# The first norm of a two-layer transformer kernel: row parts by TensorE and VectorE in turn, bias rows ahead of x, four units tile by tile

## What is computed

```python
cond = jax.nn.silu(c)                                     # (1, 1024)
mod = (cond @ ada_w[l] + ada_b[l]).reshape(B, 3, 3, 1, D) # shift, scale, gate of 3 sublayers
h = rms_norm(x, norm_g[l, 0]) * (1 + mod[:, 0, 1]) + mod[:, 0, 0]
a, b = jnp.split(h @ ffn1_w13[l], 2, axis=-1)
x = x + 0.5 * mod[:, 0, 2] * ((jax.nn.silu(a) * b) @ ffn1_w2[l])
wl = jnp.einsum("bqhd,bkd->bhqk", qb, kwb) + t5_table[t5_bucket(wd)].transpose(2, 0, 1)
```

## Time and profile before

| | |
|---|---|
| Median of three runs | 3389.39 us |
| Profiled execution | 3389.15 us, span 3387.4 us |
| TensorE | 98% of the span busy |
| VectorE, ScalarE, GpSimd | 67%, 39%, 13% |
| DMA | 380.90 MB, mean 112 GB/s |
| Granted TensorE clock | 0.997 of full |

### The profile page before, as it was taken

The page is one execution under the profiler, slowest core; times in us unless marked ns, Lnnn a source line. Parts: engine busy times, 40 slices in busy tenths (PEclk is TensorE's granted clock), DMA queues, the critical chain, the costliest instruction groups (busy, mean ns, idle before and its releaser), DMA issues. The chain is left out here.

```text
span 3387.4 us, 51035 instructions
## 1 busy us (share of the span) xinstructions
PE 3329.7 (98%) x19808; PEld 2811.7 (83%) x19808; DVE 2267.5 (67%) x3615; ACT 1317.6 (39%) x2095; POOL 438.0 (13%) x329
## 2 busy tenths in 40 slices
PE   8999999999999999999999999999999999999999
PEld 7989877788888898987778888886888888788887
DVE  6877757658775677785765877657666525766642
ACT  5424344535333433334453523243443324443321
POOL 2000200222000300020022200121200011120002
PEclk9999999999999999999999999999999999999999
DMA  6463523113542345442201353321233332223332
GB/s 252 148 229 129 166 86 94 32 39 127 176 145 96 112 154 211 144 150 88 87 26 54 128 192 124 101 77 52 81 99 99 105 102 63 68 82 94 96 104 85
DMA packets 88629, 380.90 MB, mean 112 GB/s; under 512 B 9774, under 2 KB 10926, under 8 KB 77192
## 3 DMA queue, kind: packets, MB, share of 16 engines
q1 hardware_dynamic: 88456, 378.52, 33.5%
HBM read 376.36 MB, written 2.12 MB: 112 GB/s over the span
## 5 line engine op out<-in xcount | busy, mean ns | idle before, releaser
L2001 DVE TENSOR_TENSOR wL<-wR,wH 128x1024 fp32r<-128x1024 f32 (+2 forms) x160 | 207.9, 1299 | 195.4 <-ACT wH L1289 195.2
L1289 ACT ACTIVATE wH<-wR 128x1024 fp32r<-128x1024 f32 (+2 forms) x158 | 175.0, 1107 | 381.3 <-PE bank L3452 305.6
L3697 PE MATMUL bank<-hH,wH 128*128 128x512 f32 x640 | 271.6, 424 | 0.0
L3566 PE MATMUL bank<-gHc,wH 128*128 128x512 f32 x660 | 256.8, 389 | 0.0
L3567 PE MATMUL bank<-gHc,wL 128*128 128x512 f32 x660 | 256.8, 389 | 0.0
L3568 PE MATMUL bank<-gLc,wH 128*128 128x512 f32 x660 | 256.7, 389 | 0.0
L3699 PE MATMUL bank<-hL,wH 128*128 128x512 f32 x640 | 251.6, 393 | 0.0
L3539 PE MATMUL bank<-hH,wH 128*128 128x512 f32 x640 | 249.7, 390 | 1.2 <-DVE wL L2057 1.2
L3698 PE MATMUL bank<-hH,wL 128*128 128x512 f32 x640 | 250.5, 391 | 0.0
L3540 PE MATMUL bank<-hH,wL 128*128 128x512 f32 x640 | 249.4, 390 | 0.0
L3541 PE MATMUL bank<-hL,wH 128*128 128x512 f32 x640 | 249.0, 389 | 0.0
(11 more groups left out here) (567 smaller groups left out, 8683.0 us busy)
## 6 DMA issues: line engine op xcount, KB each, us to landing
RW<-in_ffn_wq SPq DMA_DIRECT2D x80, 1024.0 KB, 5.6
adaw<-in_ada_w SPq DMA_DIRECT2D x144, 512.0 KB, 4.4
wR<-in_w_up SPq DMA_DIRECT2D x88, 512.0 KB, 3.6
wR<-in_ffn_w SPq DMA_DIRECT2D x56, 704.0 KB, 4.1
wR<-in_w_mix SPq DMA_DIRECT2D x72, 512.0 KB, 3.6
wR<-in_w_down SPq DMA_DIRECT2D x32, 704.0 KB, 4.1
wR<-in_w_in SPq DMA_DIRECT2D x40, 512.0 KB, 3.6
ada<-in_ada_first SPq DMA_DIRECT2D x8, 1024.0 KB, 12.1
```

Of the source, the lines that this page charges most:

```text
L3566: pe.matmul(o, wh[:, k, :], gHc[:, k, c], start=k == 0, stop=False)
L3697: pe.matmul(o, wH[n][:, k, :], hH[:, k, :], start=k == 0, stop=False)
```

## The change

The order of the queue: constants and `cond`, the small tensors, and only then x and the parameters; parts 0 and 1, units 0 and 1, part 2, the bias rows, parts 3 and 4, unit 2, part 5, unit 3, part 7, the first quarter, `SKEW`, part 6, the second quarter, `CSKEW`. The bias rows are made before x is transposed. Of the eight parts TensorE sums four (0, 2, 4, 6) and VectorE four (1, 3, 5, 7). TensorE's way is `part_sums` (eight matmuls of 32 rows out by 256 columns, four of them beside each other in PSUM), a copy by ScalarE, and `part_columns` (two matmuls of one column). VectorE adds squares in pairs, so that TensorE makes four row sums of 512 columns instead of sixteen of 256, and copies half of the transposed x. The norm goes tile by tile, over all 512 positions, each with its own bias and scale; the products of all four units follow tile by tile. The table matmuls stand between tiles 5 and 6. The fillers are gone. On ScalarE `sum_high(0)` moves behind the copies for the first quarter.

```diff
@@ SyncE
-            sp.dma_start(xin[:, :, :], a["x"].rearrange("(t p) d -> p t d", p=P)).then_inc(S.x_in, 16)
             sp.dma_start(cond[:, :], bc(a["c"], [P, D])).then_inc(S.const_in, 16)
...
             sp.dma_start(FLIP[:, :], a["c_flip"]).then_inc(S.tab_in, 16)
+            sp.dma_start(xin[:, :, :], a["x"].rearrange("(t p) d -> p t d", p=P)).then_inc(S.x_in, 16)
+            sp.dma_start(par[:, 0:C_END1], a["par1"][0]).then_inc(S.par_in, 16)
...
+                    ada_part(5)
+                    unit(ubase + 3, w13[l, 3], KT, 1)
+                    ada_part(7)
+                    sp.wait_ge(S.dc, 2)
+                    pair(f, 0, wq, l)
+                    sp.wait_ge(S.bias_out, 32)
+                    sp.wait_ge(S.ada0_done, 1)
+                    sp.dma_start(SKEW[:, :, :], bass.AP(bias_dram.tensor, 0, [[1, P], [640, H], [1, T]])).then_inc(S.skew_in, 16)
+                    ada_part(6)
+                    sp.wait_ge(S.ada0_done, 2)
+                    pair(f, 1, wq, l)
+                    sp.wait_ge(S.dc, 4)
                     sp.wait_ge(S.ada0_done, 4)
-                elif f:
...
+                    sp.wait_ge(S.skew_in, 16)
                     sp.dma_start(CSKEW[:, :, :], bass.AP(cbias_dram.tensor, 0, [[1, P], [1056, H], [1, 896]])).then_inc(S.skew_in, 16)
@@ ScalarE
+                first_high(0)
+                first_high(1)
+                first_sums(0)
+                act.wait_ge(S.ms, 1)
+                act.activation(rstd[:, :], bank[MS_BANK[0]][:, :], ACT.Ln, bias=eps, scale=1.0 / D).then_inc(S.ln, 2)
...
+                act.activation(rstd[:, :], rstd[:, :], ACT.Exp, scale=-0.5).then_inc(S.rstd, 2)
+                first_sums(1)
+                for k in range(KT):
+                    for e, c in enumerate(HALVES):
+                        act.wait_ge(S.hf, 2 * k + e + 1)
+                        act.activation(hH[:, k, c], HB[e][k // TT][:, k % TT, :], ACT.Identity,
+                                       bias=mod[:, k:k + 1]).then_inc(S.h_hi, 1)
+                    if k == 1:
+                        first_high(2)
+                    if k == 2:
+                        first_sums(2)
+                    if k == 4:
+                        first_high(3, fourth)
+                    if k == 5:
+                        first_sums(3)
+                        bias_tables()
@@ VectorE
+                for i in range(TT - 1):
+                    square_pair(i)
+                first(FIRST_DVE[0])
+                square_pair(TT - 1)
+                low(0)
+                low(1)
...
+                part(0)
+                part(1)
+                normed(0)
+                normed(1)
+                normed_low(0)
+                normed_low(1)
+                part(2)
+                normed(2)
+                normed_low(2)
+                first(3)
...
+                part(6)
+                normed(6)
+                first(7)
+                normed_low(6)
+                part(7)
+                normed(7)
+                normed_low(7)
@@ TensorE
+            pe.wait_ge(S.ct, 2)
+            pe.wait_ge(S.bias_sb, 1)
             pe.wait_ge(S.x_in, 16)
...
+            def part_sums(i):
...
+                for r in range(2):
+                    for g in range(4):
+                        mm = pe.matmul(bank[DS_BANK[i % 2]][32 * g:32 * (g + 1), 0:2 * P], CT[:, 4 * r + g, :], rows[:, 4 * r + g, :],
+                                       start=r == 0, stop=r == 1)
...
+            part_sums(0)
+            for i in range(TT):
+                pe.wait_ge(S.sq_sum, i + 1)
+                mm = pe.matmul(bank[MS_BANK[0]][:, :], ones, squares[2 * i], start=i == 0, stop=i == TT - 1)
+            mm.then_inc(S.ms, 2)
+            part_columns(0)
+            part_sums(1)
+            pe.wait_ge(S.rstd, 2)
+            part_columns(1)
...
+                both(0)
+                both(1)
+                part_sums(2)
+                both(2)
+                part_columns(2)
+                both(3)
+                pe.wait_ge(S.w_lo, 3)
+                tiles(2, 0, 4)
+                both(4)
+                tiles(2, 4, 5)
+                part_sums(3)
+                both(5)
+                part_columns(3)
+                pe.wait_ge(S.mod0, 2 * FIRST_PE[3] + 1)
+                bias_tables()
+                pe.wait_ge(S.w_lo, 4)
+                tiles(2, 5, 6)
+                tiles(3, 0, 6)
+                both(6)
+                both(7)
+                tiles(2, 6, 8)
+                tiles(3, 6, 8)
...
-                    warm(24)
-                    pe.wait_ge(S.mod_set, at(S.mod_set, 2))
-                    warm(3)
```

More of the change, by code:

```diff
@@ L333 @@
 SUMS = slice(3 * P, 3 * P + TT)
-ADA_PARTS = tuple((2 * c, 2 * c + 2) for c in range(KT))
+FIRST_TILES = (26, 30, 34, 38, 8, 12)
+FIRST_PE = (0, 2, 4, 6)
+FIRST_DVE = (1, 3, 5, 7)
 FIRST_COUNTS = {"w_in0": 688, "w_in1": 688, "w_hi": 86, "w_lo": 86, "w_used": 86, "sil": 4, "g_mul": 4, "g_hi": 44,
@@ L1162, in ffn @@
             def ffn(f, ubase, udn, l, w13, wq, w2, n, c, c_end):
[L1164 to L1170, removed]
+                if f == 0 and l == 0:
+                    for k in range(2):
+                        ada_part(k)
+                    for k in range(2):
+                        sp.dma_start(wR[k][:, 0:KT, :], w13[l, k]).then_inc(S.w_in[k], 16)
+                    ada_part(2)
                     sp.wait_ge(S.bias_sb, 1)
@@ L2166, in chunk, with ffn @@
                 g_low(f, q1)
-            def ffn(f, sub, n, ubase, udn, gates, ahead, part, rest=None):
+            def ffn(f, sub, n, ubase, udn, gates, ahead, part, rest=None, start=False):
                 def pair_out(i, b):
@@ new lines, in part_columns @@
+            def part_columns(i):
+                if i == 0:
+                    pe.wait_ge(S.picks, 2)
+                if i >= 2:
+                    pe.wait_ge(S.mod0, 2 * FIRST_PE[i - 2] + 1)
+                pe.wait_ge(S.ds, 2 * i + 2)
+                for j in range(2):
+                    mm = pe.matmul(bank[DC_BANK[i % 2]][:, j:j + 1], DS[i % 2][:, j * P:(j + 1) * P], picks[:, :], start=True, stop=True)
+                mm.then_inc(S.dc, 1)
+            pe.wait_ge(S.x_copied, TT)
+            pe.wait_ge(S.x_moved, TT)
@@ L3477, in open_three, with first_four, part, tiles @@
                         part(2, e, k)
+            def first_four():
+                def part(u, k):
+                    wh, wl = FIRST_W[u] if u < 3 else next(w for k0, k1, w in fourth if k0 <= k < k1)
+                    j = k if u < 3 else next(k - k0 for k0, k1, w in fourth if k0 <= k < k1)
+                    o = bank[u][:, :]
+                    pe.matmul(o, wh[:, j, :], hH[:, k, :], start=k == 0, stop=False)
+                    pe.matmul(o, wl[:, j, :], hH[:, k, :], start=False, stop=False)
+                    mm = pe.matmul(o, wh[:, j, :], hL[:, k, :], start=False, stop=k == KT - 1)
+                    if k == KT - 1:
+                        mm.then_inc(S.w_used, 1)
+                def tiles(u, k0, k1):
+                    for k in range(k0, k1):
+                        pe.wait_ge(S.h_lo, 2 * k + 2)
+                        part(u, k)
+                def both(k):
+                    tiles(0, k, k + 1)
+                    tiles(1, k, k + 1)
+                pe.wait_ge(S.w_lo, 2)
+                both(0)
[20 more added lines that the diff above has]
+                tiles(3, 6, 8)
             def products_third(o):
@@ L3569, in rows, with chunk @@
                 return mm
-            def chunk(f, u, half, xdone, xbase, ss=None):
+            def chunk(f, u, half, xdone, xbase, ss=None, between=None):
                 if half:
@@ L3578, in chunk @@
                 else:
+                    if between:
+                        pe.wait_ge(S.bm_set, H)
                     classical(f, 0)
```

312 lines of the change are left out of this document (208 added, 104 removed).

## The result

The changed kernel takes 3398.2 us (median of 8 runs, 3395.9 to 3400.3) where the kernel before takes 3388.9: a ratio of 1.0028, 95% interval 1.0017 to 1.0038. It is 9.3 us slower, and 7.6 us above the forecast of 3390.6.

A forecast was written before the change was run, and what follows sets the result against it. TensorE's stream of matmuls, busy 98%, was taken as the bound. `classical(1)` at 78.9 plus 1.7 and 2.0 for half clock gave 82.6 against 81.36, 1.2 us longer: median 3390.6 us, range 3384.0 to 3397.0.

The forecast's parts named there:

- a hole before `classical(1)` that hangs on the late table: TensorE idle ahead of `classical(1)` while GpSimd's bias copies and block sums wait for `CSKEW`: 5.7 us, sign 4 to 7.
- half clock behind the hole: TensorE after the idle stretch before `classical(1)`: three us at half clock, 1.7 us of work lost on the path.
- the other clock losses: TensorE gaps after the bias rows, before the first product and at tile 3: 2.0 us together, 0 and 5 as ends.
- the tail: From the third block sum's end (73.2) to `classical(1)` (78.9): 3.9 us of ScalarE and VectorE steps plus 1.8 for slowing.
- I take 0.6 us for each of three: Slowing of three VectorE operations beside GpSimd before `classical(1)`: 0.6 us each, 0 and 1.7 as ends.
- the table's way: `CSKEW` from issue at 52.4, behind `first(7)`, to landing at 59.8; 6.5 us as lower, 8.6 as upper end.
- The transposes at 11.84 ran at full clock after nothing: TensorE's start in the kernel before: claimed that the trace does not bear out a throttled array at the start.
- The second rival: TensorE's clock stays at half through the tiles, so `first(7)` and all behind slip by 9, not 2: 3397.6 us; chance 0.14.
- Serial part sums: `part_sums` on TensorE running in sequence, 3.4 us each instead of 1.05; slow side near 3397.6, within its chance of 0.14.
- The first rival: Before `classical(1)`: the `CSKEW` chain does not bind, TensorE's own stream sets the end, 8.2 us earlier: 3381.2; chance 0.08.
- The marker: Start of `classical(1)`, 81.36 before, 78.9 forecast: code behind it is the same, so what its start moves, the time moves.

## Why the prediction was wrong, step by step

The mechanism was the one forecast: a hole before `classical(1)` that hangs on the late table. Its size was not.

| step | forecast | measured |
|---|---|---|
| bias rows on TensorE | 2.9 us | 5.8 (8.17 to 13.99) |
| transposes begin | 13.3 | 15.9 |
| first product | 30.5 | 32.3 |
| `classical(0)` | 62.3 | 65.7 |
| `part_sums` | 1.05 us | 1.07 |
| `CSKEW` issued, landed | 52.4, 59.8 | 55.4, 62.0 |
| copies and first block sum | 7.4 us | 9.3 (62.08 to 71.39) |
| next two block sums, end | 6.0 us, 73.2 | 5.5, 76.95 |
| from there to `classical(1)` | 5.7 us | 11.2 (76.95 to 88.17) |
| TensorE done with `classical(0)` | 73.2 | 77.8 |
| `classical(1)` | 78.9 | 88.2 |
| half clock behind the hole | 1.7 us | 1.8 to 2.0 |
| the other clock losses, added to the end | 2.0 us | contained in the steps above |

The forecast's sum of 82.6 answers to 88.17 + 2.0 = 90.1 now, 7.5 us more. The table landed 2.2 late, for which 2.0 had been charged: 0.2. The copies and sums add 1.5, the tail 5.5, the clock 0.3.

**The step that failed** is "I take 0.6 us for each of three" for operations of VectorE beside GpSimd, with 1.7 as the end: 1.8 us were charged for what measured 7.3 (11.2 less the 3.9 of the operations' own lengths). Behind the third block sum's end at 76.95 stood 1.1 us of the `tL` of 74.66, which was still waiting, the four `tL` of `sum_low(1)` with 6.7, the `tL` of `sum_low(2)` with 2.2, and the first `wL` of `group1(1)` with 1.2. The forecast counted the four as one operation; each of the four waited.

The length of such a wait can be worked out: the operation ends its own length after the GpSimd instruction in progress. GpSimd's sum that starts at 69.00 ends at 71.39; 0.69 more is 72.08, and `gLc` ended at 71.93. The sum at 84.46 ends at 85.90; 1.22 more is 87.12, and the last `tL` ended at 86.98. The Trainium skill states this (SBUF — State Buffer, section "SBUF: two separate sides"): the port pair that GpSimd and VectorE share is an exclusive lock, held for a whole instruction, which a VectorE operation with two inputs from SBUF needs when the GpSimd instruction reads SBUF. The rows agree: in the kernel before, a `gf`, with one input from PSUM, keeps its 0.68 beside the block sums that begin at 61.62, where the `gLc` behind it, with two inputs from SBUF, takes 1.48 for 0.69:

```profile
62.55 0.68 DVE L2176 TENSOR_TENSOR gf<-bank,sil 128x512 f32<-128x512 f32 x1
```

It could be read from the rows of before: in the earlier trace rows the 1.22 us operation at 59.67 took 2.95 and ended at 62.62, and by the earlier trace rows the sum beside it had ended by 61.62, when the next one began. I saw the 2.95 and priced it as an accident that an operation has or has not; since GpSimd works without a pause in the new order, all of them have it but the last. Worse, I counted GpSimd's work only to the third block sum. The fourth and the weight sums, until 85.90, stood beside the tail too: in the kernel before they are separated from it by GpSimd's rest.

The 1.5 us of the copies and sums are 2.0 more for the copies, 0.1 less for the first sum and 0.4 less for the next two. The copies, of 0.15 us each, hardly slow VectorE (a `gLc` at 66.15, beside them, took 0.73) but are slowed by it: 4.85 us alone, 6.88 here, 12.1 to 15.0 where VectorE was busy all the time.

**The range.** Its upper end was added up wrongly. With the ends that the forecast itself names, 1.7 for each of the three operations (3.3 more), 5 for the clock (3.0 more) and 8.6 for the table's way (1.2 more), 82.6 becomes 90.1, 8.7 above the kernel before and not 6.5. That this is the measured 90.1 is chance: the tail exceeded its end (9.0) by 2.2, and of the 5 for the other clock losses nothing came on top of the steps.

**The bias rows.** "The transposes at 11.84 ran at full clock after nothing" was wrong. I read it in the column of the granted clock. In the changed kernel's trace that column prints full clock at 12 to 13 while matmuls of the same rows take 1.87 us (8.17) for the 1.01 of the row at 19.06:

```profile
12.00:13.00 1.00, 1.00 (x3) 0.22 (x2) 0.00 (x0) 0.00 (x0) 0.00 (x0) 1.00 1.05 439
```

The transposes of the kernel before show it themselves, with 6 records in 1 us at first and 10 later, at a printed 1.00 both times:

```profile
13.00:14.00 1.00, 1.00 (x6) 1.00 (x5) 0.00 (x0) 0.74 (x3) 0.00 (x0) 1.00 1.03 430
...
17.00:18.00 1.00, 1.00 (x10) 0.99 (x8) 0.53 (x2) 0.74 (x3) 0.00 (x0) 1.00 1.01 418
```

So TensorE starts at 1.2 GHz, and in these traces the column prints 1.00 ahead of the first change that it has. This is what the Trainium skill says (TensorE: Matmul & The Clock Gate, Part 1: the default is throttled) and what I had dismissed. It cost 2.9 us at the rows; the transposes began 2.6 late, the first product 1.8.

**The second rival**, half clock through the tiles, gave 3397.6 with a chance of 0.14. Its figure is near the result and its mechanism isn't it: filling the gap at tile 3 gained 0.6 us, and `classical(0)` was 65.72, not 71. Serial part sums are refuted by 1.07 us. The first rival is refuted by the wait in GpSimd's first row.

**The marker** held: from `strassen(2)` to the end of the span 3295.2 us before and 3296.1 after.

## What to carry to other kernels

Moving a helper engine's work later moves more than its results: ask which operations of the other engines will now run beside it. On VectorE and GpSimd an operation with two SBUF operands costs its own length plus what is left of GpSimd's instruction in progress (in one case here, what was left of four short ones), so a chain that alternates between the two should be priced at the sum of both, and rests of GpSimd are worth keeping where VectorE is on the path. Work with a distant deadline (here the bias copies, for which nothing on the path waits until `classical(3)`) goes behind what the path needs, above all when its input becomes late.

## What the runs showed of the hardware that I had not expected

- VectorE's operations with two SBUF operands beside GpSimd: 0.69 to 2.79 and 2.88, 1.22 to 3.41, 1.67 to 6.78 us; with GpSimd still, 0.69, 1.22 and 1.66 again. Shorter GpSimd instructions shortened most of VectorE's waits and lengthened GpSimd's own time (5.53 to 7.44).
- 32 small copies on GpSimd: 4.85 us alone, 13.92 beside a busy VectorE, whose operations kept their own lengths (`tL` 1.22, four `tL` 1.68).
- TensorE at half speed for all of its first 8.8 us with work, 5.8 of them matmuls of 33 rows depth, while the column of the granted clock printed 1.00.
- Eight part sums of 32 rows by 256 columns, four beside each other, took 1.07 us; the forecast's figure for a sequence of them was 3.4.
